# Rotary sums made in place on 128 partitions and carried to the heads' rows by DMAs, on one Trainium2 core

## The chip, the cores and the metric

One core of a Trainium2 chip. The metric is the device time of one execution in microseconds. The kernel before takes 1430.77 us, the median of 3 runs (1430.03 to 1432.64).

## The reference, cut to what matters

One inference step of a two-layer streaming encoder, 512 prompt frames and 32 sample frames of width 1024. In each layer a normalised input is projected by one matrix to the inputs of three parallel head groups: retention (4 heads of 64), gated linear attention (4 heads of 64) and band attention (8 heads of 64). Their outputs are joined, projected back and added; an MLP of width 4096 follows. The change touches only the rotary embedding of retention's q and k:

```python
def rotary(x, pos):
    half = HEAD_DIM // 2
    ...
    x1, x2 = x[..., :half], x[..., half:]
    return jnp.concatenate([x1 * cos - x2 * sin, x1 * sin + x2 * cos], axis=-1)

qa = rotary(heads(qa), pos)
ka = rotary(heads(ka), pos) * scale
```

## The kernel before

Activations lie transposed: features on the partitions, the T = 544 frames (512 + 32) along the row. A weight matrix is cut into units of 128 output features, 100 for each layer. Each unit's 512 KB are loaded by SyncE's queue (SP) into one of four buffers `raw`; ScalarE (ACT) makes the high part `whi` (`split(n)`, L467), VectorE (DVE) the low part `wlo` (`rest(n)`, L767), and TensorE (PE) makes 48 matmuls (hi by hi, hi by lo, lo by hi; 8 slices of the contraction; two halves of 272 frames) into two PSUM banks. `unit_out(n)` on DVE then reads the banks. DVE, ACT and PE each run the written order of `SLOTS`: slot (n, half) is half a unit of projection products on PE, and the small matmuls of the head groups (`PE_STEPS`) are put ahead of or between them. On each engine instructions run in the order in which they are written, and all order between engines is by semaphores written by hand. `begin(n)` on PE waits for `w_lo` of unit n and for the reads of units up to n - 2.

Units 6 and 7 (`RK`) are retention's k, units 8 and 9 (`RQ`) its q. The weight columns are permuted so that the first unit of a pair holds the first halves (x1) of all four heads, 32 rows for each head, and the second unit the second halves (x2). `unit_out(RK)` writes `rot[0]` = x1 cos and `rot[1]` = x1 sin, `unit_out(RK + 1)` writes `sq[0]` = x2 sin and `sq[1]` = x2 cos, all on 128 partitions. `rotary(first, g)` (L852 to L864) then makes the sums, and because the matmuls of the heads want each head's 64 features on adjacent rows (`rk`, `rq`, two heads for each g), it does so in four DVE operations of 32 partitions for each g: 8 for k after `rest(9)` (slots (8, 0) and (8, 1)), 8 for q after `rest(11)` (slots (10, 0) and (10, 1)), so 16 for each layer. Since `rot` and `sq` are used again for q, `unit_out(RQ)` waits for `rot_ready` 2. The readers of `rk` and `rq`: the step ("diag", RET) at PE's slot (11, 1), which waits for `rot_ready` 4; DVE's decay scaling (L961, L963); the transposes and the state steps after it.

DVE's work around it, in its written order: slot (8, 0): `unit_out(7)`, the last level of the gated linear attention (GLA), `rest(9)` and rotary of k; slot (9, 0): `unit_out(8)` (writes `rot`), `rest(10)`; slot (9, 1): step ("kv", GLA), 16 state updates (L1017) and 2 for the sample frames (L1023); slot (10, 0): `unit_out(9)` (writes `sq`), `rest(11)`, rotary of q; slot (10, 1): the adds of ("out", GLA) (L1031); slot (11, 0): `unit_out(10)`, ("out_s", GLA), `rest(12)`; slot (11, 1): ("diag", RET), L947 on. PE's step ("out", GLA) at slot (10, 1) takes all four side banks; bank 2 of them comes free with `state_s_ready`, after the second L1023.

SP issues the loads in order: `load(m)` waits for `rest(m - 4)`. Between loads stand other transfers (`between`): before `load(15)` `states_out(GLA)` (4 stores of 32 KB), before `load(16)` `state_in(RET)` (2 loads of 32 KB that wait for DVE's `outs_dve`), and so on; `band_in(0)` waits for `rot_ready` 4.

Of the kernel before, what the change touches and what calls it, by code (L numbers as in the profile page):

```python
# [11 lines left out]
T = TP + TS  # L12
# [24 lines left out]
ALU, ACT = mybir.AluOpType, mybir.ActivationFunctionType  # L37
# [4 lines left out]
GK, GQ, GV, RK, RQ, RV, AQ, GATE = 0, 2, 4, 6, 8, 10, 12, 24  # L42

GLA, RET = 0, 1
# [28 lines left out]
    _steps[(12, 0)] = _steps[(12, 0)] + [("gn", GLA)]  # L73
    _steps[(15, 0)] = [("gn", RET)]
GN_PARTS = [(0, 8), (8, 20)]
ROTARY = {(8, 0): (RK, 0), (8, 1): (RK, 1), (10, 0): (RQ, 0), (10, 1): (RQ, 1)}
for _u in range(4):
    _b = 16 + 3 * _u
    DVE_STEPS[(_b + 1, 0)] = [("norm", _u, 0), ("score", _u, 1)]
# [7 lines left out]
for _steps in (DVE_STEPS, ACT_STEPS):  # L87
# [10 lines left out]
    qk_dve=6, pe_lev=6, lev_read=6, pe_diag=2, diag_read=2, qe_act=1, qe_dve=1, kd_arg=1, kd_act=1, kd_ready=1,  # L98
    dec_ready=1, pe_tok=4, tok_read=4, pe_kv=2, state_ready=32, state_s_ready=4, pe_out=2, out_act=2, out_dve=4,
    pe_out_s=2, outs_act=2, outs_dve=4, centred=2, gn_var=2, gn_act=6, gn_done=4, pe_back=2, back_read=4,  # L100
    rot_ready=4, ret_scaled=2, o_cleared=1, s_cleared=1, part_hi=8, part_lo=8, pe_heads=4, heads_act=4,
    pe_score=8, score_dve=32, max_ready=8, exp_done=8, norm_done=8, pe_score_s=4, score_s_dve=8, exp_s=4,
    norm_s=4, pe_turn=8, turned=24, pe_turn_s=4, turned_s=4, pe_pv=4, pv_act=4, pv_dve=4, pe_pv_s=4, pvs_act=4,
    pvs_dve=4, gate_act=8, gate_dve=8, cat_dve=4, cat_hi=4, cat_lo=4, relu_ready=32, z_hi=32, z_lo=32,
# [43 lines left out]
def hybrid_encoder(nc, x, wu, w_low, a2, small, bias, bias_s, st_ret, st_gla, ck, cv,  # L148
# [3 lines left out]
    with ctx:  # L152
# [22 lines left out]
        sq = [sb(f"sq{i}", [P, T]) for i in range(2)]  # L175
# [35 lines left out]
        rot = [at("rot0", [P, T], arena + Z), at("rot1", [P, T], arena + Z + 4 * T)]  # L211
        rv, rk, rq = (at(n, [P, PW], arena + (2 + i) * Z) for i, n in enumerate(["rv", "rk", "rq"]))
# [33 lines left out]
        sems = {}  # L246

        def sem(name):
# [17 lines left out]
            "pe_diag", "diag_read", "qe_act", "qe_dve", "kd_arg", "kd_act", "kd_ready", "dec_ready",  # L266
            "pe_tok", "tok_read", "pe_kv", "state_ready", "state_s_ready", "pe_out", "out_act", "out_dve",
            "pe_out_s", "outs_act", "outs_dve", "centred", "gn_var", "gn_act", "gn_done",
            "pe_back", "back_read", "rot_ready", "ret_scaled", "o_cleared", "s_cleared",
            "part_hi", "part_lo", "pe_heads", "heads_act", "pe_score", "score_dve", "max_ready", "exp_done", "norm_done",  # L270
            "pe_score_s", "score_s_dve", "exp_s", "norm_s", "pe_turn", "turned", "pe_turn_s", "turned_s",
            "pe_pv", "pv_act", "pv_dve", "pe_pv_s", "pvs_act", "pvs_dve",
# [7 lines left out]
        with nc.Block() as block:  # L280
            @block.sync
            def _(sp):
# [12 lines left out]
                for layer in range(L):  # L295
                    nth = counter(layer)
# [19 lines left out]
                    def band_in(u):  # L316

                        if u == 0:
                            sp.wait_ge(sems["rot_ready"], nth("rot_ready", 4))
                            sp.wait_ge(sems["pe_tok"], nth("pe_tok", 4))  # L320
                        for p in range(2):
                            if u >= 1:
                                sp.wait_ge(sems["score_dve"], nth("score_dve", 4 * (2 * (u - 1) + p + 1)))
                            sp.dma_start(Bh[p][:, :], bias[layer, 2 * u + p, :, :]).then_inc(sems[f"bias_in{p}"], 16)
                        if u >= 2:
                            sp.wait_ge(sems["pe_score_s"], nth("pe_score_s", u - 1))
                            sp.wait_ge(sems["pe_pv_s"], nth("pe_pv_s", u - 1))
                        cols = slice(u * P, (u + 1) * P)
                        sp.dma_start(kct[u % 2][:, :], ck[layer, u, :, :]).then_inc(sems[f"cache_in{u % 2}"], 16)
                        sp.dma_start(cvb[u % 2][:, :, :], cv[layer, :, cols].rearrange("(j p) c -> p j c", p=P)) \  # L330
                            .then_inc(sems[f"cache_in{u % 2}"], 16)
                        if u >= 1:
                            sp.wait_ge(sems["score_s_dve"], nth("score_s_dve", 2 * u))
                        sp.dma_start(Bs[:, :], bias_s[layer, u, :, :]).then_inc(sems["bias_s_in"], 16)

                    def states_out(kind):
                        sp.wait_ge(sems["state_ready"], nth("state_ready", 16 * (kind + 1)))
# [6 lines left out]
                    def rows_out(u):  # L344
# [9 lines left out]
                    load(RAW)  # L354
                    state_in(GLA)

                    between = {11: (states_out, GLA), 12: (state_in, RET), 14: (states_out, RET), 15: (band_in, 0),
                               17: (rows_out, 0), 18: (band_in, 1), 20: (rows_out, 1), 21: (band_in, 2),
                               23: (rows_out, 2), 24: (band_in, 3), 26: (rows_out, 3)}
                    for n in range(RAW + 1, N_IN + RAW):  # L360
# [388 lines left out]
            def _(dve):  # L749
# [7 lines left out]
                for layer in range(L):  # L757
                    nth = counter(layer)
# [51 lines left out]
                    def unit_out(n):  # L810
# [4 lines left out]
                            dve.wait_ge(sems["rstd_ready"], nth("rstd_ready", 1))  # L815

                        if n == RQ:
                            dve.wait_ge(sems["rot_ready"], nth("rot_ready", 2))

                        def out(dst, by):  # L820
                            return nc.vector.tensor_tensor(dst, src, by, ALU.mult)
# [1 line left out]
                        if n in (GQ, GQ + 1):  # L823
                            d = gq[:, (n - GQ) * T:(n - GQ + 1) * T].rearrange("p (a b) -> p a b", a=2)
                            ins = nc.vector.scalar_tensor_tensor(d, src, HD ** -0.5, halves(rstd), ALU.mult, ALU.mult)
                        elif n in (RK, RQ):
# [4 lines left out]
                            ins = out(halves(rot[1]), halves(nt[1]))  # L831
                        elif n in (RK + 1, RQ + 1):
                            link(out(halves(sq[0]), halves(nt[1])))
                            ins = out(halves(sq[1]), halves(nt[0]))
                        elif n >= GATE:
                            ins = out(halves(G[n - GATE]), halves(rstd))
                        elif n >= AQ:
# [4 lines left out]
                            if which == 0:  # L842
                                ins = nc.vector.scalar_tensor_tensor(d, src, HD ** -0.5, halves(rstd), ALU.mult, ALU.mult)
                            else:
                                ins = out(d, halves(rstd))
# [3 lines left out]
                                      halves(rstd))  # L849
                        ins.then_inc(sems["unit_read"], 1)  # L850

                    def rotary(first, g):  # L852

                        dst = rk if first == RK else rq
                        if layer and first == RK and g == 0:
                            for s in range(2):
                                dve.wait_ge(sems[f"stored{s}"], nth(f"stored{s}", 0))
                        dve.wait_ge(sems["unit_read"], nth("unit_read", first + 2))
                        c = slice(g * T, (g + 1) * T)
                        for p in range(2):  # L860
                            s32 = slice(32 * (2 * g + p), 32 * (2 * g + p) + 32)
                            nc.vector.tensor_tensor(dst[64 * p:64 * p + 32, c], rot[0][s32, :], sq[0][s32, :], ALU.subtract)
                            ins = nc.vector.tensor_tensor(dst[64 * p + 32:64 * p + 64, c], rot[1][s32, :],
                                                          sq[1][s32, :], ALU.add)  # L864
                        ins.then_inc(sems["rot_ready"], 1)

                    def square_sums(a, b):
                        return nc.vector.reduce_sum(gst[0][:, a:b], osq[:, a * HD:b * HD].rearrange("p (a c) -> p a c", c=HD),
# [277 lines left out]
                    for n, half in SLOTS:  # L1146
                        if half == 0 and n >= 3 and n != 15:
                            unit_out(n - 1)
                        rest_first = n == 14
                        if half == 0 and rest_first:  # L1150
                            rest(n + 1)
                        for st in DVE_STEPS.get((n, half), []):
                            stage(st)
                        if (n, half) == (15, 0):
                            unit_out(n - 1)
                        if half == 0 and not rest_first:
                            rest(n + 1)
                        if (n, half) in ROTARY:
                            rotary(*ROTARY[(n, half)])
                        if half == 0 and n > GATE + 1:  # L1160
                            gate_rest(n - GATE - 2)
                        if half == 1 and n > GATE:
                            gate_min(n - GATE - 1)
                            gate_mul(n - GATE - 1)
# [116 lines left out]
            def _(pe):  # L1281
# [6 lines left out]
                for layer in range(L):  # L1288
# [47 lines left out]
                    def stage(st, quarter=0):  # L1336
# [26 lines left out]
                        elif what == "diag":  # L1363
# [1 line left out]
                            q, k = ((gq, gk), (rq, rk))[kind]  # L1365
                            pe.wait_ge(sems["unit_read"], nth("unit_read", GQ + 2)) \
                                if kind == GLA else \
                                pe.wait_ge(sems["rot_ready"], nth("rot_ready", 4))
                            take(0, 1, 2, 3)
                            for p, g, c in chunks():  # L1370
                                r, o = slice(64 * p, 64 * p + 64), g * T + c * CH
# [411 lines left out]
```

## Time and profile before

| | us |
|---|---|
| median of 3 runs (range) | 1430.77 (1430.03 to 1432.64) |
| the profiled execution | 1430.05 |
| its span, first to last instruction | 1428.2 |
| PE busy | 1400.8 (98%) |
| DVE busy | 773.3 (54%) |
| ACT busy | 521.0 (36%) |
| POOL busy | 147.2 (10%) |

All times are microseconds from the start of the span unless marked ns. L862 is line 862 of the kernel before. PEld is PE's weight load, which runs beside its matmuls; SPq is SP's queue as it issues DMAs. Matmuls are pipelined: in a steady stream one starts every 0.12 to 0.13 us though each is shown for 0.29 us. Both layers have the same stretch, layer 0 from about 85 to 120 us and layer 1 from about 785 to 820 us; the first is read unless it says otherwise.

### The profile page before, as it was taken

The page shows a single profiled execution, that of the slowest core. Times are in us where ns is not written, and L with a number is a line of the kernel's source. Part 1 is how long each engine was busy: PE and PEld are TensorE (multiplying, and loading weights), DVE is VectorE, ACT ScalarE, POOL GpSimd, SP SyncE. Part 2 cuts the span into 40 slices and gives each one's busy share as a digit, 9 for nine tenths or more (in the row PEclk, how much of TensorE's full clock was granted, in tenths as well). Part 3 has the DMA queues.
Part 4 walks back from the last instruction along what each step waited for, and adds up shares of the span by engine and source line. Part 5 has one row for each costly group of instructions (what it writes and reads, how often), then busy time and mean ns, then how long its engine had stood idle before and what let it go on. Part 6 is the DMA issues. An engine that isn't in the chain of part 4 may idle for free.

```text
span 1428.2 us, 28637 instructions
## 1 busy us (share of the span) xinstructions
PE 1400.8 (98%) x12590; PEld 1359.4 (95%) x12590; DVE 773.3 (54%) x1224; ACT 521.0 (36%) x859; POOL 147.2 (10%) x107
## 2 busy tenths in 40 slices
PE   8999999999999999999999999999999999999996
PEld 8999889899999999999998999889999999999996
DVE  6797766744434334344767967765453443433433
ACT  5323556633213223123332236565332231321331
POOL 0200000031020110200202000001301102002012
PEclk9999999999999999999999999999999999999998
DMA  6123333222222222222221223422222222222211
GB/s 231 59 59 101 98 111 100 75 99 85 85 88 89 90 89 89 89 89 89 78 73 46 66 83 117 137 89 75 89 89 90 89 86 84 86 86 89 89 60 63
DMA packets 50635, 127.82 MB, mean 90 GB/s; under 512 B 8400, under 2 KB 17744, under 8 KB 50512
## 3 DMA queue, kind: packets, MB, share of 16 engines
q1 hardware_dynamic: 50224, 125.44, 27.0%
q8 instruction: 100, 1.64, 0.5%
q10 hardware_dynamic: 288, 0.55, 0.1%
q14 instruction: 23, 0.19, 0.0%
HBM read 118.77 MB, written 7.21 MB: 88 GB/s over the span
## 4 chain that ended last, share of the span: by engine, by line
PE 87%; DVE 5%; ACT 3%; issue 3%; POOL 1%; DMA 0%; POOLq 0%; SPq 0%; DVEq 0%; ACTq 0%
PE PS L1302 85%; ACT whi L467 1%; POOL h L435 1%; PE PS L1537 1%; ACT Pr L594 1%; PE PS L1416 1%; DVE Pr L1084 0%; DMA raw<-in_wu 0%; DVE F L889 0%; DVE gb L935 0%; DVE Pr L1096 0%; DVE sq L1203 0%; DVE wlo L767 0%; ACT xhi L470 0%; DVE O L877 0%
## 5 line engine op out<-in xcount | busy, mean ns | idle before, releaser
L1302 PE MATMUL PS<-xhi,whi 128*128 128x272 f32 x1920 | 562.9, 293 | 3.5 <-DVE wlo L767 2.6
L1302 PE MATMUL PS<-xhi,wlo 128*128 128x272 f32 x1920 | 555.2, 289 | 0.0
L1302 PE MATMUL PS<-xlo,whi 128*128 128x272 f32 x1920 | 552.7, 288 | 0.0
L767 DVE TENSOR_TENSOR wlo<-raw,whi 128x1024 fp32r<-128x1024 f32 x200 | 251.6, 1258 | 386.0 <-ACT whi L467 385.3
L467 ACT ACTIVATE whi<-raw 128x1024 fp32r<-128x1024 f32 x200 | 211.6, 1059 | 558.6 <-PE PS L1302 554.0
L1302 PEld LDWEIGHTS PS<-xhi,whi 128*128 128x128 f32 x1920 | 361.3, 188 | 15.5 <-issue 9.0
L1302 PE MATMUL PS<-zhi,wlo 128*128 128x272 f32 x1280 | 370.6, 290 | 0.0
L1302 PE MATMUL PS<-zhi,whi 128*128 128x272 f32 x1280 | 368.5, 288 | 0.4 <-DVE wlo L767 0.4
L1302 PE MATMUL PS<-zlo,whi 128*128 128x272 f32 x1280 | 368.5, 288 | 0.0
L1302 PEld LDWEIGHTS PS<-xlo,whi 128*128 128x128 f32 x1920 | 361.8, 188 | 0.2
L1302 PEld LDWEIGHTS PS<-xhi,wlo 128*128 128x128 f32 x1920 | 361.2, 188 | 0.0
L1302 PEld LDWEIGHTS PS<-zhi,whi 128*128 128x128 f32 x1280 | 241.0, 188 | 0.9 <-DVE wlo L767 0.9
L1302 PEld LDWEIGHTS PS<-zlo,whi 128*128 128x128 f32 x1280 | 241.1, 188 | 0.0
L1302 PEld LDWEIGHTS PS<-zhi,wlo 128*128 128x128 f32 x1280 | 240.8, 188 | 0.0
L435 POOL TENSOR_TENSOR h<-h,sq 128x544 f32<-128x544 f32 x62 | 89.3, 1441 | 653.1 <-DVE sq L1203 653.1
L662 ACT ACTIVATE zhi<-nt 128x544 fp32r<-128x544 f32 x64 | 42.2, 659 | 90.6 <-DVE nt L1192 90.6
L1195 DVE TENSOR_TENSOR zlo<-nt,zhi 128x544 fp32r<-128x544 f32 x64 | 50.0, 781 | 46.4 <-ACT zhi L662 46.4
L1203 DVE TENSOR_TENSOR sq<-PS,r 128x544 f32<-128x544 f32 x62 | 44.5, 718 | 20.6 <-PE PS L1302 14.5
L594 ACT ACTIVATE Pr<-Pr,mx 128x128 f32<-128x128 f32 (+1 forms) x64 | 35.2, 552 | 34.9 <-DVE mx L1089 34.9
L1192 DVE SCALAR_TENSOR_TENSOR nt<-PS,nt 128x544 f32<-128x544 f32 x64 | 46.0, 718 | 0.0
L426 POOL TENSOR_SCALAR ssum<-sq 128x544 f32<-128x544 f32 x2 | 2.4, 1183 | 416.9 <-ACT sq L651 416.9
L659 ACT ACTIVATE nt<-PS 128x544 f32<-128x544 f32 x64 | 38.8, 606 | 0.0
(226 smaller groups left out, 1083.0 us busy)
## 6 DMA issues: line engine op xcount, KB each, us to landing
raw<-in_wu SPq DMA_DIRECT2D x199, 512.0 KB, 3.5
Bh<-in_bias SPq DMA_DIRECT2D x16, 256.0 KB, 3.9
h<-in_x SPq DMA_DIRECT2D x8, 272.0 KB, 6.1
out_k_t<-att_k SPq DMA_DIRECT2D x8, 272.0 KB, 4.3
out_y_t<-y SPq DMA_DIRECT2D x8, 272.0 KB, 2.7
kct<-in_ck SPq DMA_DIRECT2D x8, 256.0 KB, 3.2
cvb<-in_cv SPq DMA_DIRECT2D x8, 256.0 KB, 5.0
out_v_p<-vtk SPq DMA_DIRECT2D x8, 256.0 KB, 2.2
```

What stands on the lines that cost most here:

```text
L435: nc.gpsimd.tensor_tensor(h[:, m, :], h[:, m, :], sq[m % 2][:, :], ALU.add) \
L467: nc.scalar.activation(whi[n % SPL][:, :], raw[n % RAW][:, :], ACT.Copy).then_inc(sems["w_hi"], 1)
L594: ins = nc.scalar.activation(r, r, ACT.Exp, bias=mx[:, p, i:i + 1], accum_out=rs[:, p, i:i + 1])
L659: nc.scalar.activation(halves(r), PS[:, 2 * (n % 2):2 * (n % 2) + 2, 0:HT], ACT.Relu) \
L662: nc.scalar.activation(zhi[:, k, :], r[:, :], ACT.Copy).then_inc(sems["z_hi"], 1)
L767: nc.vector.tensor_tensor(wlo[n % SPL][:, :], raw[n % RAW][:, :], f32(whi[n % SPL][:, :]), ALU.subtract).then_inc(sems["w_lo"], 1)
L1192: nc.vector.scalar_tensor_tensor(halves(r), PS[:, 2 * (n % 2):2 * (n % 2) + 2, 0:HT], 0.0, halves(r), ALU.max, ALU.mult).then_inc(sems["un ...
L1195: nc.vector.tensor_tensor(zlo[:, k, :], r[:, :], f32(zhi[:, k, :]), ALU.subtract) \
L1203: nc.vector.tensor_tensor(halves(sq[m % 2]), PS[:, 2 * (n % 2):2 * (n % 2) + 2, 0:HT], halves(r2), ALU.mult).then_inc(sems["unit_read"], 1)
L1302: return nc.tensor.matmul(out, lhsT, rhs, start=start, stop=stop, skip_group_check=True)
L1416: nc.tensor.transpose(PS[:, M0 + g, i * P:(i + 1) * P], src[:, g * T + i * P:g * T + (i + 1) * P], ident[:, :])
L1537: last = nc.tensor.transpose(PS[:, M0 + b, c:c + P], Pr[p][:, P_OFF[i] + j * P:P_OFF[i] + (j + 1) * P], ident[:, :])
```

## The change

Rotary of k is one call in slot (8, 0) and rotary of q one call in slot (10, 0). Each is two DVE operations on all 128 partitions, in place in `rot[0]` and `rot[1]`, that count `rot_sum`. A new step of SP, `heads_apart`, waits for `rot_sum` and issues 8 DMAs from SBUF to SBUF, each of 32 partitions by 544 elements of float32 (68 KB), from `rot[x]` to `rk` or `rq`; each adds 16 to `rot_in`. For k it stands before `load(14)`, for q before `load(16)`; `state_in(RET)` moves from before `load(16)` to before `load(17)`. `unit_out(RQ)` on DVE now waits for `rot_in` 128 (all of k's carries), ("diag", RET) on PE and `band_in(0)` on SP for `rot_in` 256. The wait for `stored0` and `stored1` in layer 1 moves from DVE to SP.

```diff
-ROTARY = {(8, 0): (RK, 0), (8, 1): (RK, 1), (10, 0): (RQ, 0), (10, 1): (RQ, 1)}
+ROTARY = {(8, 0): RK, (10, 0): RQ}
...
+                    def heads_apart(first):
+
+                        sp.wait_ge(sems["rot_sum"], nth("rot_sum", 1 + (first == RQ)))
+                        if layer and first == RK:
+                            for s in range(2):
+                                sp.wait_ge(sems[f"stored{s}"], nth(f"stored{s}", 0))
+                        dst = rk if first == RK else rq
+                        for g in range(2):
+                            for p in range(2):
+                                for x in range(2):
+                                    sp.dma_start(dst[64 * p + 32 * x:64 * p + 32 * x + 32, g * T:(g + 1) * T],
+                                                 rot[x][32 * (2 * g + p):32 * (2 * g + p) + 32, :]).then_inc(sems["rot_in"], 16)
...
-                    between = {11: (states_out, GLA), 12: (state_in, RET), 14: (states_out, RET), 15: (band_in, 0),
+                    between = {10: (heads_apart, RK), 11: (states_out, GLA), 12: (heads_apart, RQ), 13: (state_in, RET), 14: (states_out, RET), 15: (band_in, 0),
...
                         if n == RQ:
-                            dve.wait_ge(sems["rot_ready"], nth("rot_ready", 2))
+                            dve.wait_ge(sems["rot_in"], nth("rot_in", 16 * 8))
...
-                    def rotary(first, g):
-
-                        dst = rk if first == RK else rq
-                        if layer and first == RK and g == 0:
-                            for s in range(2):
-                                dve.wait_ge(sems[f"stored{s}"], nth(f"stored{s}", 0))
+                    def rotary(first):
+
                         dve.wait_ge(sems["unit_read"], nth("unit_read", first + 2))
-                        c = slice(g * T, (g + 1) * T)
-                        for p in range(2):
-                            s32 = slice(32 * (2 * g + p), 32 * (2 * g + p) + 32)
-                            nc.vector.tensor_tensor(dst[64 * p:64 * p + 32, c], rot[0][s32, :], sq[0][s32, :], ALU.subtract)
-                            ins = nc.vector.tensor_tensor(dst[64 * p + 32:64 * p + 64, c], rot[1][s32, :],
-                                                          sq[1][s32, :], ALU.add)
-                        ins.then_inc(sems["rot_ready"], 1)
+                        nc.vector.tensor_tensor(rot[0][:, :], rot[0][:, :], sq[0][:, :], ALU.subtract)
+                        nc.vector.tensor_tensor(rot[1][:, :], rot[1][:, :], sq[1][:, :], ALU.add) \
+                            .then_inc(sems["rot_sum"], 1)
...
                                 if kind == GLA else \
-                                pe.wait_ge(sems["rot_ready"], nth("rot_ready", 4))
+                                pe.wait_ge(sems["rot_in"], nth("rot_in", 16 * 16))
```

## Rows read from the trace of the kernel before

**Rows 1.** The page: busy time (share of the span, instructions), and the chain's shares by engine.
```profile
PE 1400.8 (98%) x12590; PEld 1359.4 (95%) x12590; DVE 773.3 (54%) x1224; ACT 521.0 (36%) x859; POOL 147.2 (10%) x107
...
PE 87%; DVE 5%; ACT 3%; issue 3%; POOL 1%; DMA 0%; POOLq 0%; SPq 0%; DVEq 0%; ACTq 0%
```

**Rows 2.** Waits of PE and PEld, 60 to 170 us: total us, times, longest.
```profile
PE PS L1488 <- DVE O L1059: 1.1, 1, 1.1
...
PEld PS L1302 <- DVE wlo L767: 0.2, 1, 0.2
PEld PS L1416 <- DVE rk L963: 0.2, 1, 0.2
PEld PS L1302 <- DVE Ps L992: 0.2, 1, 0.2
```

**Rows 3.** Timeline of DVE: start us, us, operation, [idle before, releaser].
```profile
89.29 1.22 DVE L767 TENSOR_TENSOR wlo<-raw,whi 128x1024 fp32r<-128x1024 f32 x1
90.43 0.71 DVE L862 TENSOR_TENSOR rk<-rot,sq 32x544 f32<-32x544 f32 x1
...
96.37 1.49 DVE L821 TENSOR_TENSOR rot<-PS,nt 128x544 f32<-128x544 f32 x2
97.77 1.22 DVE L767 TENSOR_TENSOR wlo<-raw,whi 128x1024 fp32r<-128x1024 f32 x1
...
101.97 0.47 DVE L1023 SCALAR_TENSOR_TENSOR Ss<-Ss,dec,PS 128x64 f32<-128x64 f32 x2
...
104.88 0.71 DVE L862 TENSOR_TENSOR rq<-rot,sq 32x544 f32<-32x544 f32 x1
...
108.00 1.29 DVE L1031 TENSOR_TENSOR O<-PS,O 128x512 f32<-128x512 f32 x2 [0.23 <-ACT O L538]
...
112.26 0.72 DVE L821 TENSOR_TENSOR rv<-PS,rstd 128x544 f32<-128x544 f32 x1
...
116.32 0.69 DVE L947 TENSOR_TENSOR Pm<-PS,dm_sb 128x512 f32<-128x512 f32 x1 [0.57 <-PE PS L1302]
```

**Rows 4.** Groups of DVE's instructions: count, busy us, mean ns, idle before.
```profile
L1139 DVE TENSOR_TENSOR G<-G,sq 128x544 f32<-128x544 f32 x8 | 5.8, 725 | 1.2 <-DVE G L1133 0.5 <-ACT sq L695 0.2
...
L863 DVE TENSOR_TENSOR rk<-rot,sq 32x544 f32<-32x544 f32 x8 | 5.7, 718 | 0.1
```

**Rows 5.** Timeline of PE and PEld at the edges of its steps.
```profile
99.83 0.19 PEld L1302 LDWEIGHTS PS<-xhi,whi 128*128 128x128 f32 x1
...
102.84 0.29 PE L1302 MATMUL PS<-xhi,wlo 128*128 128x272 f32 x1
103.06 0.45 PE L1302 MATMUL PS<-vtok,Pm 64*64 64x64 f32 x8
...
114.10 1.03 PE L1302 MATMUL PS<-rq,rk 64*64 64x64 f32 x28
```

**Rows 6.** Timeline of SP's queue: issues of DMAs.
```profile
102.53 0.35 SPq L341 DMA_DIRECT2D out_gla_p<-S  x1
102.92 0.43 SPq L342 DMA_DIRECT2D out_gla_s<-Ss  x1
103.39 0.44 SPq L341 DMA_DIRECT2D out_gla_p<-S  x1
```

**Rows 7.** DMA issues: count, KB of each, median us from issue to landing.
```profile
raw<-in_wu SPq DMA_DIRECT2D x199, 512.0 KB, 3.5
out_k_t<-att_k SPq DMA_DIRECT2D x8, 272.0 KB, 4.3
...
out_gla_p<-S SPq DMA_DIRECT2D x4, 32.0 KB, 1.5
...
out_v_s<-vtk SPq DMA_DIRECT2D x8, 16.0 KB, 2.0
```

**Rows 8.** Windows of 1 us; the last two columns are DMA share and GB/s.
```profile
93.00:94.00 1.00, 1.00 (x10) 1.00 (x10) 0.97 (x2) 0.74 (x3) 0.00 (x0) 1.00 0.75 307
94.00:95.00 1.00, 1.00 (x11) 1.00 (x10) 0.97 (x3) 0.00 (x0) 0.00 (x0) 1.00 0.05 20
```

**Rows 9.** Timeline of PE in layer 1, the first matmul of ("out", GLA).
```profile
802.77 0.44 PE L1302 MATMUL PS<-vtok,Pm 64*64 64x64 f32 x7
```

More of the change, by code:

```diff
@@ L100 @@
     pe_out_s=2, outs_act=2, outs_dve=4, centred=2, gn_var=2, gn_act=6, gn_done=4, pe_back=2, back_read=4,
-    rot_ready=4, ret_scaled=2, o_cleared=1, s_cleared=1, part_hi=8, part_lo=8, pe_heads=4, heads_act=4,
+    rot_sum=2, rot_in=256, ret_scaled=2, o_cleared=1, s_cleared=1, part_hi=8, part_lo=8, pe_heads=4, heads_act=4,
     pe_score=8, score_dve=32, max_ready=8, exp_done=8, norm_done=8, pe_score_s=4, score_s_dve=8, exp_s=4,
@@ L268, in hybrid_encoder @@
             "pe_out_s", "outs_act", "outs_dve", "centred", "gn_var", "gn_act", "gn_done",
-            "pe_back", "back_read", "rot_ready", "ret_scaled", "o_cleared", "s_cleared",
+            "pe_back", "back_read", "rot_sum", "rot_in", "ret_scaled", "o_cleared", "s_cleared",
             "part_hi", "part_lo", "pe_heads", "heads_act", "pe_score", "score_dve", "max_ready", "exp_done", "norm_done",
@@ L318, in band_in @@
                         if u == 0:
-                            sp.wait_ge(sems["rot_ready"], nth("rot_ready", 4))
+                            sp.wait_ge(sems["rot_in"], nth("rot_in", 16 * 16))
                             sp.wait_ge(sems["pe_tok"], nth("pe_tok", 4))
@@ L1158, in _ @@
                         if (n, half) in ROTARY:
-                            rotary(*ROTARY[(n, half)])
+                            rotary(ROTARY[(n, half)])
                         if half == 0 and n > GATE + 1:
```

## The prediction

> **What bounds the kernel now.** I read the page's busy times and its chain first: PE is busy 98% of the span, its weight loads 95%, and 87% of the chain that ended last is PE's own [rows 1]. So time comes off only where PE waits, and is added wherever PE is made to wait. Next I read PE's waits around the place of the change: from 60 to 170 us PE lacks only 1.1 us (L1488, for DVE's L1059 at 154 us), and PEld three times 0.2 us [rows 2]. None of these is a wait for `rk` or `rq` as rotary leaves them; the 0.2 us of L1416 is for the scaling by decay, a chain that starts at PE's own diag step. DVE is another matter: it works almost without a gap from 85 us until 115.8 us, and is level with PE again only at 116.32, where L947 has stood idle 0.57 us for PE [rows 3]. DVE is thus late in this stretch, but its lateness reaches PE almost nowhere. The question is not what DVE saves but how late the two new waits are against PE's dates.
>
> **The sums.** An operation on 32 partitions takes 718 ns; one on 128 partitions with both inputs in SBUF, the shape of the new sums, 725 ns [rows 4]. Rotary goes from 8 x 0.72 = 5.7 us to 2 x 0.72 = 1.4 us, so 4.3 us less each time, and 4 x 4.3 = 17 us less DVE busy time in two layers (773 to about 756). On PE's path this is worth nothing by itself: DVE has no successor there that starts sooner than PE lets it, because from 116.32 on DVE waits for PE in either case. As a bound from below the gain can't exceed what PEld lacks of DVE in this stretch, 0.2 + 0.2 + 0.2 = 0.6 us a layer [rows 2], 1.2 us in all; I take 0, since two of the three stand before the rotary sums or behind PE's own diag step.
>
> **The wait of DVE for k's carries.** This is the term that decides. Before, `unit_out(8)` started at 96.37, directly behind the last of the 8 operations [rows 3]. After:
> - `rest(9)` and the start of the sums stay: 90.43. The sums end at 90.43 + 1.44 = 91.87, and SP, which has just issued `load(13)`, can start at about 91.90.
> - SP issues 8 DMAs. The second follows the first by 0.39 us, later ones by 0.47 us [rows 6]: the eighth is issued at 91.90 + 0.39 + 6 x 0.475 = 95.14.
> - Landing of a transfer from SBUF to SBUF isn't in the trace. The nearest rows: 1.5 us for a store of 32 KB, 2.0 us for a store from 32 partitions, 3.5 us for a load of 512 KB, 4.3 us for a store of 272 KB [rows 7]. I take 2.0 (same partitions, small), with 1.5 and 4.3 as ends. The eighth lands at 97.14 (96.64 to 99.44).
>
> So `unit_out(8)` starts d = 0.8 us later than before (0.3 to 3.1), although DVE has 4.3 us less to do: its gain has become idle time, and somewhat more.
>
> Behind the waiting `unit_out(8)` are queued on DVE `rest(10)`, the 18 state updates, `unit_out(9)` and `rest(11)`. Who waits for them, and with what slack:
> - PE's `begin(10)` needs `rest(10)`, which ended at 97.77 + 1.22 = 98.99; PEld starts the unit at 99.83 [rows 3, 5]. Slack 0.8 us.
> - PE's ("out", GLA) takes bank 2, which is free when the L1023 pair ends, 101.97 + 0.47 = 102.44. The last matmul ahead of it starts at 102.84, and the step at 103.06 [rows 3, 5]. The 0.22 between these is also there ahead of steps that wait for nothing, so the slack is 103.0 - 102.44, about 0.55 us with some 0.05 for the semaphore taken off. This one binds.
>
> PE's stall is then d - 0.55: 0.25 us in each layer for d = 0.8, 0 for d = 0.3, 2.55 for d = 3.1. A shift here stays, since PE is never ahead of itself again. Layer 1 has the same stretch (its step starts at 802.77 [rows 9]; that layer's L1023 pair ends as far ahead of it), so 0.5 us in all (0 to 5.1).
>
> **q's carries.** `rest(11)` ended and the sums began at 104.88 [rows 3]; with d they begin at 105.7 and end at 107.1. `load(15)` and the 4 stores of `states_out` are out by then. SP issues 8 DMAs, the last at 107.15 + 3.24 = 110.4; at 2.0 us they land at 112.4. PE's diag wants them at 114.10 [rows 5]: slack 1.7 us, so nothing. With 4.3 us of landing and d = 3.1, they land at 117.0, when PE itself has slipped to 116.65: 0.35 us more a layer, which makes the upper end 5.8 us. On DVE the L1031 adds at 108.00 wait for ACT [rows 3] and lie behind sums that now end before them.
>
> **The rest of what moves.** `load(14)` is now issued behind the 8 carries, at 99.8 at the latest (it waits for `rest(10)` in any case, formerly 99.0), and `load(16)` behind q's, which are issued by 111; it waits for `rest(12)`, now as before, and that comes at 113 to 115.8. Loads are four units ahead and take 3.5 us [rows 7], so ACT's split isn't reached. `state_in(RET)` goes out after `load(16)`, not before; its data are wanted at about 132 us by the RET state update, 15 us later. `band_in(0)` waits for carries that PE has needed 20 us earlier. The wait for `stored` in layer 1 is for stores of layer 0, long done. The 32 carries move 2.2 MB beside 127.8 MB. All of it is hidden by that distance; cost 0.
>
> **Sum.** Profiled execution 1430.05 + 0 (sums) + 0.5 (k's carries) + 0 (q's carries) + 0 (rest) = 1430.55. That execution lies 0.7 below the median of the runs shown, and carried to the median the forecast is 1431.3 us: no change that can be measured, 0.2% of this time (2.9 us) being about the least that a measurement can tell from none.
>
> **Rivals.**
> 1. *The carries are served slowly, and queue behind the load.* `load(13)` is issued at 90.54, and its data keep the DMA engines busy until 94.05 [rows 8]; by then five carries are issued. A load reaches 307 GB/s in a full microsecond. If transfers of 32 partitions get half of that, the 544 KB of eight carries take 3.6 us from 94.05, to 97.7, and with about 0.7 us of completion (half of the 1.5 us of a small store) the last lands at 98.4: d = 2.0, stall 1.45 a layer, 2.9 us in all, 1433.7. For it speaks that the load's data do lie just ahead; against it, that the eighth carry is issued a microsecond after the load is through. The Trainium skill has such a rule (SBUF — State Buffer, "Door 1: The DMA port swizzle"): a transfer over partitions 0 to 31 reaches 8 of the 16 DMA ports, 189 GB/s at 1 MiB where all partitions give 328. By that page's rate the eight take 2.9 us from 94.05, so an estimate of 97.0 for the data and of 97.7 for the landing: 0.8 us stall a layer, a total of 1.6 us. No transfer of 32 partitions of this size is in the trace, so no row can say whether it holds.
> 2. *Slower: every carry lands like a large transfer.* If the time from issue to landing is 3.4 us or more, whatever the size, the end is at 98.5 or later, d above 2.0, and both layers together lose more than 2.9 us: at 4.3 us of landing 5.8 us, 1436.6. It decides from 3.4 us on. Against it: all stores of small size land in 1.5 to 2.0 us [rows 7]; for it: a store of rows of 2176 bytes, as the carries have, took 4.3.
> 3. *Faster.* DVE's early finish would have to reach PE. Between 85 and 116 us PE lacks no more than 0.6 us of anything from DVE [rows 2], so 1.2 us at most, which would be 1429.6, if k's carries also cost nothing (landing at 1.5 us, d = 0.3). This can't be told from no change.
> 4. *The change doesn't do what it says*: the DVE operations on 128 partitions cost more than 0.72 us. [Rows 4] all but rule it out; DVE would have to lose 4 us more to matter.
>
> **How the numbers follow.** Forecast (0 to 1.5 us more) 0.58; rival 1 (1.5 to 3.3 more) 0.20; rival 2 0.12; rival 3, a little faster, 0.09; rival 4 0.01. Half of rival 1's upper part, some 0.05, passes 2.9 us. Faster by over 0.2% would need a mechanism that no row shows, or a shift of medians: 0.03. Slower: 0.12 + 0.05 = 0.17. Same: 0.80. The range reaches from rival 3, less a part of the 0.7 us by which the lowest run lies under the median, 1429.3, to the upper part of rival 1, 1434.2; what it leaves out is rival 2 and some of both tails.
>
> **What would show it.** DVE idle of 4 to 6 us ahead of L821 `rot` (`unit_out(8)`), with a DMA `rk<-rot` as releaser, at about 92 and 792 us; rot at 96.7 to 97.7 and not 96.37; the carries 0.47 us apart on SP; a wait of PEld or PE of about 0.25 us at the first `vtok,Pm` matmul of each layer for DVE's L1023, and none at the diag step; DVE busy near 756 us. The prediction is wrong if a carry takes over 3.4 us to land, if SP issues such a DMA in more than 0.6 us, or if PE has a wait for `rot_in`.

## The result

The changed kernel takes 1436.25 us, the median of 6 runs (1435.14 to 1438.51); before, 6 runs on the same chip gave 1430.44 (1430.03 to 1432.64). The ratio is 1.0039, 95% interval 1.0026 to 1.0052: 5.6 us slower (the medians themselves differ by 5.8). In a second set, 7 runs of the changed kernel gave 1435.11 against 1430.56, ratio 1.0032 (1.0021 to 1.0043). The forecast was 1431.3 with a range to 1434.2: both the size and "no change" were wrong. The time lies where rival 2 had put its own, though it came about in another way.

The page of the kernel after, the lines that answer to [rows 1]:

```profile
PE 1403.5 (98%) x12590; PEld 1361.9 (95%) x12590; DVE 756.2 (53%) x1200; ACT 521.0 (36%) x859; POOL 147.2 (10%) x107
...
PE 85%; DVE 6%; issue 3%; ACT 3%; POOL 1%; DMA 1%; SPq 1%; POOLq 0%; DVEq 0%; ACTq 0%
```

DVE's busy time fell by 17.1 us, as worked out, and SP's queue and a DMA have come into the chain, with 1% each. The profiled execution took 1435.70 us, its span 1433.9. PE's waits from 60 to 170 us, which answer to [rows 2] (total, times, longest):

```profile
PE PS L1307 <- DVE wlo L780: 1.9, 1, 1.9
PE PS L1493 <- DVE O L1064: 1.3, 2, 1.1
PE PS L1307 <- DVE Ss L1028: 0.3, 1, 0.3
```

The first and the last are new; the middle one (L1064, the L1059 of the kernel before) was there. L780 is the `rest` of the kernel before (L767), L1028 its L1023. The timeline of DVE in the kernel after, which answers to [rows 3]:

```profile
90.06 1.22 DVE L780 TENSOR_TENSOR wlo<-raw,whi 128x1024 fp32r<-128x1024 f32 x1
91.19 0.72 DVE L868 TENSOR_TENSOR rot<-rot,sq 128x544 f32<-128x544 f32 x1
91.83 0.72 DVE L869 TENSOR_TENSOR rot<-rot,sq 128x544 f32<-128x544 f32 x1
100.15 1.48 DVE L834 TENSOR_TENSOR rot<-PS,nt 128x544 f32<-128x544 f32 x2 [7.60 <-DMA rk<-rot]
101.55 1.22 DVE L780 TENSOR_TENSOR wlo<-raw,whi 128x1024 fp32r<-128x1024 f32 x1
...
119.64 0.69 DVE L952 TENSOR_TENSOR Pm<-PS,dm_sb 128x512 f32<-128x512 f32 x1 [1.82 <-PE PS L1307]
```

The stretch begins with `rest(9)`, at 90.06 here and at 89.29 before. So I count from `rest(9)`: the first q unit is read (`rot<-PS`) 10.09 us after it; before it was 96.37 - 89.29 = 7.08. DVE is d = 3.01 us late, not 0.8. The diag step's result (`Pm<-PS`), which only follows PE, comes 29.58 us after `rest(9)`; before it was 27.03. The stretch costs 2.55 us. In layer 1 the same three instants are:

```profile
792.28 1.22 DVE L780 TENSOR_TENSOR wlo<-raw,whi 128x1024 fp32r<-128x1024 f32 x1
...
801.57 1.48 DVE L834 TENSOR_TENSOR rot<-PS,nt 128x544 f32<-128x544 f32 x2 [6.80 <-DMA rk<-rot]
...
821.06 0.69 DVE L952 TENSOR_TENSOR Pm<-PS,dm_sb 128x512 f32<-128x512 f32 x1 [1.83 <-PE PS L1307]
```

d = 9.29 - 7.08 = 2.21, and the cost 28.78 - 27.07 = 1.71 us. Together these are 4.26 of the 5.7 us of span. Where d comes from is in SP's queue, which answers to [rows 6], and in the chain, whose rows are start, us, what:

```profile
92.58 5.05 SPq L346 DMA_DIRECT2D rk<-rot  x8
```

```profile
96.39 0.59 SPq L346
96.98 0.04 issue
97.03 3.03 DMA rk<-rot
```

An issue takes 0.59 us, 0.635 from one to the next, where stores had taken 0.43 and 0.475. (In layer 1 the eight take 5.22 us, with one pause of 0.36 us between two of them.) And the last carry of layer 0 needs 3.03 us to land, while the median of all is the 2.0 us that I had assumed (an answer to [rows 7]):

```profile
rk<-rot SPq DMA_DIRECT2D x16, 68.0 KB, 2.0
rq<-rot SPq DMA_DIRECT2D x16, 68.0 KB, 2.0
```

### The profile page after: what moved, and what is told of

Its sections match the earlier page's. It is cut to its first block, busy times and chain, and to the rows that moved or that the text cites. A ratio compares the mean times of both kernels' runs of the same rounds, so it can differ in the third digit from the quotient of the medians.

```text
span 1433.9 us, 28645 instructions
## 1 busy us (share of the span) xinstructions
PE 1403.5 (98%) x12590; PEld 1361.9 (95%) x12590; DVE 756.2 (53%) x1200; ACT 521.0 (36%) x859; POOL 147.2 (10%) x107
## 4 chain that ended last, share of the span: by engine, by line
PE 85%; DVE 6%; issue 3%; ACT 3%; POOL 1%; DMA 1%; SPq 1%; POOLq 0%; DVEq 0%; ACTq 0%
PE PS L1307 83%; ACT whi L480 1%; POOL h L448 1%; PE PS L1542 1%; ACT Pr L607 1%; DVE wlo L780 1%; SPq L346 1%; DVE Pr L1089 0%; DVE S L1022 0%; DMA rk<-rot 0%; DVE F L894 0%; DVE gb L940 0%; DMA sm<-in_small 0%; ACT xhi L483 0%; DVE Pr L1101 0%
## 5 line engine op out<-in xcount | busy, mean ns | idle before, releaser
L780 DVE TENSOR_TENSOR wlo<-raw,whi 128x1024 fp32r<-128x1024 f32 x200 | 251.6, 1258 | 385.9 <-ACT whi L480 385.2
```

Source lines behind the costliest of these rows:

```text
L780: nc.vector.tensor_tensor(wlo[n % SPL][:, :], raw[n % RAW][:, :], f32(whi[n % SPL][:, :]), ALU.subtract).then_inc(sems["w_lo"], 1)
```

## The experiments

The theory (A): DVE's wait for k's eight carries makes its later work late, and PE waits for that; the largest part of DVE's wait is the number of issues times 0.63 us. Against it stood B (part of the loss is at the start and the end of the program), C (the carries' traffic, or their issues ahead of the loads, cost in themselves) and the prediction's rival 1 (the carries queue behind the load's data).

### The kernel before, once more

No edit.

> The kernel before, unchanged, to see how far two programs with the same text differ, and whether its start and end vary. In the profiles of before and after, 4.25 us of the 5.7 us of span lie in the two rotary stretches; 0.8 us lie ahead of 40 us and 0.65 us behind 1400 us, where the granted clock was 0.87 (10 to 20 us) and 0.73 (from 1400 us) against 1.00 and 0.77. Theory A (the wait for k's carries is the whole cause, the rest is variation of the profiled executions): a new profile of before shows starts or ends that differ by several tenths of a us again; time 1430.0 to 1432.6. Theory B (start and end are part of the change): start and end come out as in the first profile to 0.1 us.

1430.79 us (11 runs, 1429.79 to 1431.50), ratio 0.9998 (0.9989 to 1.0006). Start and end came out within 0.3 us of the first profile; `rest(9)` at 89.41. This by itself decides little about B; `q_only`, below, decides more.

### The wait taken away, the carries kept

```diff
+        rotq = [qkv[1][0], qkv[1][2]]
...
-                            dve.wait_ge(sems["rot_in"], nth("rot_in", 16 * 8))
...
-                            link(out(halves(rot[0]), halves(nt[0])))
-                            ins = out(halves(rot[1]), halves(nt[1]))
+                            ro = rot if n == RK else rotq
+                            link(out(halves(ro[0]), halves(nt[0])))
+                            ins = out(halves(ro[1]), halves(nt[1]))
```

> As after, but q's sums lie in two tiles of their own (the band attention's q and v tiles of the second set, idle at this time), so unit_out of the first q unit waits for no carry; all 32 carries are still made. Theory A (the wait of DVE for k's eight carries makes the loss, by rest(10) and the state updates arriving late at PE): DVE starts that unit_out some 1 us after the sums, not 8; both waits of PE in each stretch vanish; 1430.4 to 1431.8 us. Theory C (the carries themselves cost: their transfers, or their issues on SP that hold up the loads of weights): the loss of 5.8 us stays, 1435 to 1437. Theory B: 1.4 us of it stays, 1432.

1430.79 us (11 runs, 1429.65 to 1431.47), ratio 0.9997 (0.9988 to 1.0006). The whole loss is gone. Here `rotq`, two tiles of the band attention that are idle at this time, takes q's products and sums. DVE and SP of this kernel:

```profile
89.65 1.22 DVE L781 TENSOR_TENSOR wlo<-raw,whi 128x1024 fp32r<-128x1024 f32 x1
...
92.06 0.72 DVE L832 TENSOR_TENSOR att_q<-PS,nt 128x544 f32<-128x544 f32 x1
...
97.33 3.16 DVE L1022 SCALAR_TENSOR_TENSOR S<-S,dec,PS 128x64 f32<-128x64 f32 x16 [2.66 <-PE PS L1307]
...
116.72 0.69 DVE L952 TENSOR_TENSOR Pm<-PS,dm_sb 128x512 f32<-128x512 f32 x1 [1.84 <-PE PS L1307]
```

```profile
92.17 5.05 SPq L347 DMA_DIRECT2D rk<-rot  x8
```

The eight carries take SP the same 5.05 us, but nobody on the path waits for them. DVE is ahead of PE now (2.66 us idle before the state updates, when it had none), and the diag result comes 27.07 us after `rest(9)`, as before (27.03). C falls with this: all 32 carries are there and cost nothing that the interval can show. DVE's 17 us less work also bring nothing: this kernel is not faster than the one before.

### Only k, only q

`k_only` makes q's rotary by the eight operations on 32 partitions again, `q_only` k's:

```diff
-ROTARY = {(8, 0): RK, (10, 0): RQ}
...
-                            rotary(ROTARY[(n, half)])
+                            (rotary if ROTARY[(n, half)] == RK else rotary32)(ROTARY[(n, half)])
```

(for `q_only` with RQ; `rotary32` is the old `rotary` for both g in one call.)

> Only k is summed in place and carried; q's rotary is made by the eight operations on 32 partitions, as before. Theory A: the whole loss is here, 1435.5 to 1437, PE's waits in each stretch as in after (2.5 and 1.7 us). Theory C: half of the loss, about 1433.3, since half of the carries are left.

> Only q is summed in place and carried; k's rotary is made as before. Theory A: no loss, 1430.0 to 1431.5; the last carry lands before PE's diag step, with some 1 to 2 us to spare (in after: last issue at 114.4, landed near 116.6, diag at 117.4). Theory C: half of the loss, about 1433.3.

`q_only`: 1430.24 us (11 runs, 1429.71 to 1432.05), ratio 0.9999 (0.9990 to 1.0007). q's carries cost nothing, as A says. `k_only`: 1442.9 us (5 runs, 1441.69 to 1446.58), ratio 1.0087 (1.0075 to 1.0100), a loss of 12 us, twice what was expected. PE's waits in it from 88 to 125 us:

```profile
PE PS L1324 <- DVE O L1053: 2.6, 1, 2.6
PE PS L1324 <- DVE wlo L781: 2.1, 1, 2.1
PE PS L1324 <- DVE Ss L1045: 0.3, 1, 0.3
```

The last two are the known ones. The first is new and was of my making: I had put all eight operations for q ahead of the adds of the "out" step, where the kernel before has four ahead of them and four behind. With this mended (`k_only_split`, the call cut in two, (10, 0) and (10, 1)):

> As k_only, but q's eight operations stand in two halves around the adds of L1053, as in the kernel before; in k_only I had put all eight ahead of the adds, and PE waited 2.6 us a layer for these adds. Only the first two waits of PE should be left: as after, 1434.5 to 1436.5 us, which would say that q's in-place sums are worth nothing in after. If they are worth something once DVE is late, it is above after: 1437 to 1442.

1435.56 us (5 runs, 1434.42 to 1436.21), ratio 1.0033 (1.0020 to 1.0045), and the wait for the adds is gone. So k alone makes the loss, and whether q's sums take 1.4 or 5.7 us makes no difference of a size that these intervals can show. The miss of `k_only` tells something all the same: with DVE 3.1 us late in layer 0 and 2.0 in layer 1, eight operations ahead of the adds cost PE 2.6 us a layer.

One thing more is in the profile of `k_only_split`. Right after PE's wait of 2.2 us in layer 0 its matmuls start 0.227 us apart from 104.2 to 107.0 us and not 0.125, and the granted clock (the third value from the end) is that of the lower level, 1.2 GHz:

```profile
104.00:105.00 1.00, 1.00 (x7) 1.00 (x6) 1.00 (x6) 0.00 (x0) 0.00 (x0) 0.54 0.90 324
105.00:106.00 1.00, 1.00 (x6) 1.00 (x6) 1.00 (x6) 0.00 (x0) 0.00 (x0) 0.50 0.32 127
```

That stretch costs 3.99 us with d = 3.31, some 1.1 us more than the lateness alone gives in the other profiles (the table below). In `k_only` the clock fell to 0.66 from 820 to 825 us, behind the wait for the adds in layer 1, where the stretch cost 1.5 us more than its waits. In the profiles of after, its repetition, `wide` and `before_load`, with waits of 1.8 to 2.5 us in the same place, it stayed at 1.00. So such a wait can be followed by a loss of clock of about 1 us, and need not be; the length of the wait alone does not decide it here.

### DVE late without a DMA

```diff
+                            if n == RQ:
+                                for t in (qkv[1][0], qkv[1][2], qkv[0][0], qkv[0][2]):
+                                    nc.vector.tensor_tensor(t[:, :], nt[0][:, :], nt[1][:, :], ALU.mult)
```

in the kernel before.

> The kernel before with four more DVE products of 128x544 (0.65 us apart, both inputs in SBUF, results unused) just ahead of the reads of the first q unit: d = 2.6 to 2.9 us and not one DMA more. Theory A (only DVE's lateness counts): the same two waits of PE as in k_only, whose d was 3.15 us, and the same third one, for L1053's adds ahead of the sample frames' step, each shorter by the difference of d: 4.8 us a layer, 9.6 in two, some 1440 us. Theory C (the carries' traffic adds to it): clearly less, since no carry is made: under 1436.

1434.72 us (8 runs, 1433.50 to 1435.86), ratio 1.0029 (1.0019 to 1.0039). The number expected was wrong, since it rested on `k_only` with its third wait; the mechanism is clearest here. The trace of this kernel:

```profile
89.33 1.22 DVE L767 TENSOR_TENSOR wlo<-raw,whi 128x1024 fp32r<-128x1024 f32 x1
...
98.95 1.48 DVE L821 TENSOR_TENSOR rot<-PS,nt 128x544 f32<-128x544 f32 x2
...
118.44 0.69 DVE L950 TENSOR_TENSOR Pm<-PS,dm_sb 128x512 f32<-128x512 f32 x1 [0.30 <-PE PS L1305]
```

```profile
PE PS L1305 <- DVE wlo L767: 1.5, 1, 1.5
PE PS L1305 <- DVE Ss L1026: 0.3, 1, 0.3
```

d = 9.62 - 7.08 = 2.54 and the stretch costs 29.11 - 27.03 = 2.08 us (2.55 and 2.16 in layer 1), with the same two waits as the kernel after. The stretches cost 4.24 us together, and the medians differ by 4.5. No carry is made: DVE's lateness is enough.

### Two queues

Half of the carries (p = 1) are issued by GpSimd's queue, with a semaphore of their own:

```diff
+                    for dst, count in ((rk, 1), (rq, 2)):
+                        pool.wait_ge(sems["rot_sum"], nth("rot_sum", count))
+                        for g in range(2):
+                            for x in range(2):
+                                nc.gpsimd.dma_start(dst[64 + 32 * x:96 + 32 * x, g * T:(g + 1) * T],
+                                                    rot[x][32 * (2 * g + 1):32 * (2 * g + 1) + 32, :]).then_inc(sems["rot_in2"], 16)
```

> As after, but half of the carries (p = 1) are issued by GpSimd's queue, which is idle at this time, and half by SP. In after an issue takes SP 0.59 us, 0.63 us from one to the next, eight of them 5.0 us. Theory A: SP's four are issued by 94.4 on before's time scale and land by 96.0; GpSimd's price for an issue is not in any trace so far. If it is 0.6 us or less, d is about 0 and the loss is gone, 1430 to 1431.5; at 1.0 us and 2.5 us of landing d is about 1.5, 1432.5. If the loss stays at 5 us or more the issue rate was not the cause, or GpSimd takes over 1.5 us for each.

1431.25 us (11 runs, 1429.78 to 1432.63), ratio 1.0005 (0.9997 to 1.0014). A twelfth execution took 2266.52 us and is left out; its mean granted clock was 0.554, where the others had 0.993 to 0.995, and why it was so low stays open. From `rest(9)` to the first q unit:

```profile
90.97 1.22 DVE L786 TENSOR_TENSOR wlo<-raw,whi 128x1024 fp32r<-128x1024 f32 x1
...
98.26 1.48 DVE L840 TENSOR_TENSOR rot<-PS,nt 128x544 f32<-128x544 f32 x2 [4.80 <-DMA rk<-rot]
```

SP issues its four in 2.51 us, GpSimd its four in 2.33. d = 7.29 - 7.08 = 0.21 us (0.39 in layer 1), and the stretches cost nothing: the wait is there, 4.80 us of it, but within the slack. Four issues fewer in a row are 2.5 us, while the median landing rose from 2.0 to 2.8 us (SP's) and 2.6 us (GpSimd's), so a part of the gain was given back. The number of issues in a row on one queue is thus the largest term, and halving it is enough.

### What an issue costs

`wide` moves 136 elements of all 128 partitions with each carry, so that the rows don't come to the heads' places and only its times are of use; `sixteen` cuts each carry in two along the row (its edit is shown):

```diff
-                                    sp.dma_start(dst[64 * p + 32 * x:64 * p + 32 * x + 32, g * T:(g + 1) * T],
-                                                 rot[x][32 * (2 * g + p):32 * (2 * g + p) + 32, :]).then_inc(sems["rot_in"], 16)
+                                    for c in (0, HT):
+                                        sp.dma_start(dst[64 * p + 32 * x:64 * p + 32 * x + 32, g * T + c:g * T + c + HT],
+                                                     rot[x][32 * (2 * g + p):32 * (2 * g + p) + 32, c:c + HT]) \
+                                            .then_inc(sems["rot_in"], 16)
```

> As after, but each of the 8 carries takes 136 elements of all 128 partitions, so the same 68 KB each and the same count; the rows do not come to the heads' places (that part of the computation is changed). If the 32-partition shape is what makes an issue take 0.59 us, it is 0.43 here, as for SP's stores, the last issue is 1.1 us sooner and the stretch loses about 1.1 us a layer less; if a transfer from SBUF to SBUF costs that, 0.59 stays.

> As after, but each carry is cut into two of 272 elements: 16 transfers of 34 KB for k and 16 for q, the same bytes. If an issue costs by the instruction, SP needs 10.1 us for k's, the last is issued at 101.3 on before's scale and lands at 103.3: d = 7, PE's first two waits grow by 4.5 to 5 us a layer, some 1445 to 1448. If it costs by the bytes, the time is that of after, 1436.

SP's queue in `wide`, then in `sixteen`:

```profile
92.66 5.05 SPq L347 DMA_DIRECT2D rk<-rot  x8
```

```profile
92.60 11.36 SPq L347 DMA_DIRECT2D rk<-rot  x16
```

The shape is not the cause: 5.05 us for eight in `wide` too (1434.72 us in one run, d = 3.41 and 2.09, costs 2.96 and 1.58). Nor are the bytes: half the size costs as much for each issue (10.05 us for sixteen in layer 1; 11.36 in layer 0, some more). So among these three shapes the price is by the instruction. `sixteen` took 1459.63 us in one run, more than expected: d = 8.14 and 6.87, but q's carries are late for PE's diag step as well, which before had slack:

```profile
PE PS L1309 <- DVE wlo L782: 7.1, 1, 7.1
PE PS L1309 <- DMA rq<-rot: 3.7, 1, 3.7
```

### The load ahead of the carries

```diff
-                    between = {10: (heads_apart, RK), 11: (states_out, GLA), ...
+                    between = {9: (heads_apart, RK), 11: (states_out, GLA), ...
```

> As after, but k's carries are issued ahead of load(13), not behind it; that load then goes out some 6 us later. In after the carries of layer 0 landed 2.0 to 2.4 us after their issue, but the last 3.0 us, and in layer 1 the first three 2.5 to 2.7 us. Rival 1 of the prediction (the carries queue behind the load's data): every carry lands in 2.0 us, d is 2.1 us in both layers, the stretches lose 3.3 us, 1434 or less. If the load ahead does not matter: as after, 1435 to 1436.5. If load(13) is now late for its split: more than after.

1435.70 us (5 runs, 1433.33 to 1436.21), ratio 1.0032 (1.0020 to 1.0045): as after. The last carry in the chain of layer 0, and of layer 1, of this kernel:

```profile
96.60 3.62 DMA rk<-rot
```

```profile
799.94 2.02 DMA rk<-rot
```

With no load ahead of it the last carry of layer 0 took 3.62 us, even more than after's 3.03, and d was 3.60 and 2.18. Rival 1 falls as the account of the late landing. Its mechanism is there, but on carries that nobody waits for: in layer 1 of after the first three carries, issued while the load's data came in, landed in 2.5 to 2.7 us, and in 2.0 us here.

What goes with the late landing is another row. DMA queues of the kernel after, in the 3 us in which the last carry of layer 0 lands (packets, MB, share of 16 engines):

```profile
q1 hardware_dynamic: 96, 0.14, 18.6%
q8 instruction: 1, 0.02, 2.3%
```

One packet of instructions takes 2.3% of 16 engines in 3 us, so 0.023 x 16 x 3 = 1.1 us of one engine. Such a packet stands in this place of layer 0 in six profiles with a last landing of 2.9 to 3.6 us; in layer 1 of the same six, where the last carry lands in 2.0 us, none does. The two go together in size as well. The packet's own time comes from its share of 16 engines in the half microsecond in which it starts, where it is counted whole: 12.4% x 16 x 0.5 us = 0.99 us in `after_again`, 21.0% and 1.68 us in `before_load`.

```profile
q8 instruction: 1, 0.02, 12.4%
```

```profile
q8 instruction: 1, 0.02, 21.0%
```

| kernel, layer 0 | packet, us of one engine | last carry's landing, us |
|---|---|---|
| after_again | 0.99 | 2.87 |
| after | 1.13 | 3.03 |
| k_only | 1.22 | 3.15 |
| wide | 1.34 | 3.42 |
| k_only_split | 1.39 | 3.33 |
| before_load | 1.68 | 3.62 |

In all six the landing is later than 2.05 us by nearly the packet's time. In a seventh profile, `own_tiles`, the packet took 0.94 us and the last carry 3.8, but there a load of 512 KB was issued right behind it. That the carry's part on that engine waits for the packet fits these rows but is an inference; no run moved the packet.

### The changed kernel, once more

> The changed kernel, unchanged. In the profiled runs so far a stretch loses d - 0.46 us (d: how much later than before DVE reads the first q unit, counted from the rest(9) ahead of it): after 3.01 and 2.21 give 2.55 and 1.71, late_dve 2.54 and 2.55 give 2.08 and 2.16, two_queues 0.21 and 0.39 give 0 and 0. Theory A with these numbers: both stretches together lose 4 to 5 us again and the median is 1434.5 to 1435.5; what is above that is variation of the carries' landing from run to run, or of the start (granted clock 0.87 or 1.00 from 10 to 20 us). If the median is again 5.8 above before's and the stretches show 4.3, some 1.5 us lie outside of the stretches and stay open.

1435.11 us (7 runs, 1433.88 to 1436.50). d = 2.86 and 2.21, costs 2.68 and 1.73, together 4.4 us against 4.55 between the medians of this set. The first of the two contains 0.2 us of PE's wait for a carry of q at the diag step, which the first profile does not have. In the first set the medians differ by 5.8 us where its profile shows 4.3; the intervals of the two sets overlap. What remains above the stretches is 0.1 to 1.5 us, and is left open. A fall of the clock like that of `k_only_split` would have the size: the six executions of the first set had mean granted clocks of 0.992 to 0.994, the seven of the second 0.993 to 0.996. Neither profile shows such a fall in the stretches, so this is not shown.

Stretches with carries or delays, in one table (layer 0; layer 1; us). `k_only` and `sixteen`, which have a third wait, and a wait for q's carries, on top, are not in it:

| kernel | d | cost | d - cost |
|---|---|---|---|
| after | 3.01; 2.21 | 2.55; 1.71 | 0.46; 0.50 |
| after_again | 2.86; 2.21 | 2.68; 1.73 | 0.18; 0.48 |
| late_dve | 2.54; 2.55 | 2.08; 2.16 | 0.46; 0.39 |
| wide | 3.41; 2.09 | 2.96; 1.58 | 0.45; 0.51 |
| before_load | 3.60; 2.18 | 3.47; 1.69 | 0.13; 0.49 |
| k_only_split | 3.31; 1.98 | 3.99; 1.49 | -0.68; 0.49 |
| two_queues | 0.21; 0.39 | 0; 0 | |

A stretch costs d less some 0.46 us. The exceptions are all in layer 0: `after_again` and `before_load` have 0.2 us at the diag step on top, where PE waits for a carry of q, and `k_only_split` has the fall of the clock.

About B: the granted clock of PE from 10 to 20 us, the third value from the end of a window's row, was 1.00 in before. In after and in `q_only` it was lower:

```profile
10.00:20.00 10.00, 10.00 (x71) 9.92 (x71) 10.00 (x17) 8.03 (x14) 0.00 (x0) 0.87 1.05 393
```

```profile
10.00:20.00 10.00, 9.31 (x61) 9.24 (x62) 10.00 (x16) 8.34 (x14) 0.00 (x0) 0.83 1.05 394
```

`rest(9)` stood at 90.06 and 90.94 against 89.29. But `q_only` is as fast as before in the median of 11 runs. The start varies between executions by more than what is in question, so the 0.77 us that lie ahead of layer 0's stretch in after's profile are not put to the change's account. The other 0.7 us of its span lie behind layer 1's stretch, towards the end of the program; in the second profile of the same kernel that part is 0.8 us shorter than in before, so it is not put to the change either. B has no support left, though a few tenths of a microsecond can't be excluded.

## Why the prediction was wrong, point by point

- **What bounds the kernel; DVE's saving is worth nothing on PE's path.** Right. DVE's busy time came out at 756.2 us as forecast, and with the wait gone (`own_tiles`) the kernel is 0.9997 of the one before.
- **The sums.** Right: 0.72 us each, 0.64 from the first's start to the second's.
- **SP's issues.** This is the step that failed, the price of an issue in the term of k's carries. I took 0.475 us between issues from stores of 128 partitions [rows 6], and kept no second value; the issue of a transfer from SBUF to SBUF takes 0.635. Seven steps took 4.45 us in place of the 3.24 in the sum, 1.2 us more; in layer 1, with its pause, 4.63 us, 1.4 more. I had given both ends to the landing but none to the issue, though the trace showed no issue of this kind either. The prediction named an issue of more than 0.6 us among what would make it wrong, without pricing it.
- **The landing.** 2.0 us was right for most carries and for the last one of layer 1; the last of layer 0 took 3.03. It was inside the bounds given for it (1.5 to 4.3), but the stated range left the upper ones out: its end, 1434.2, is reached when d is about 2.3 us in both layers, and d came out at 3.01 and 2.21.
- **The slack.** 0.55 us was forecast, 0.46 measured, at the same place: the L1023 pair and bank 2, with `begin(10)` taking the larger part of the wait since it comes first on PE. With the measured d (3.01 and 2.21) and my slack the sum would have been 2.46 + 1.66 = 4.1 us, and the stretches show 4.26. The mechanism was right, and the term of k's carries was mis-sized: 0.5 us forecast, 4.3 measured.
- **The sum of two shortages.** The forecast's d of 0.8 us had already used up the slack of 0.55, so all that came on top counted in full, once for each layer: 1.2 + 1.4 us of issues and 1.0 us of landing in layer 0 make 3.6 of the 3.8 us missed.
- **q's carries.** Worked out as free with 1.7 us to spare; they are free or cost 0.2 us (a wait of PE for `rot_in` at the diag step in layer 0 of one of the two profiles of the changed kernel, and in `before_load`), because DVE and with it the sums were later than forecast. `q_only` shows no loss.
- **The rest of what moves.** Right: no load was late in the stretches; `state_in(RET)` behind `load(16)` made no wait.
- **Rivals.** Rival 2 (slower) gave the right sign with the wrong cause: it wanted a landing of 3.4 us or more, and in the changed kernel the latest took 3.03 and most 2.0; what it said of a d above 2 us holds. Rival 1's load ahead is refuted by `before_load`. The rule of the Trainium skill cited beside it, that a transfer over 32 partitions reaches half of the ports (SBUF — State Buffer, "Door 1: The DMA port swizzle"), can't be seen here: carries of all 128 partitions (`wide`) landed in the same median of 2.0 us, and with 68 KB every 0.635 us, 110 GB/s, the issues set the pace, below the 189 GB/s of that rule. A chance of 0.17 for slower was too small, because both terms of the wait, the issue and the landing, came from rows of another kind of transfer, and only the landing had been given bounds.

## What to carry to other kernels

A wait for several DMAs issued in a row costs the number of issues times the time of one issue, plus the landing of the last; price the issue from a transfer of the same kind (SBUF to SBUF here 0.635 us, stores 0.475), and give it bounds if the trace has none. Give the last landing bounds too: it is one transfer, not the median, and here it took 2.0 to 3.6 us. When an engine off the path is slowed down, look for the smallest slack among all that is queued behind the new wait: from there on every tenth counts in full, once for each layer. If a transfer's source must be written again soon, there are two ways to try: another tile for the next writer took the transfers off the path here, and splitting the issues over two queues brought them within the slack; the saving on DVE, for which PE does not wait, brought nothing in either case.

## What the runs showed of the hardware that I had not expected

- The issue of a DMA from SBUF to SBUF holds SP for 0.59 to 0.60 us, whether it moves 68 KB or 34 KB, 32 partitions or 128 (after, `sixteen`, `wide`); a store of 128 partitions 0.43.
- The last of k's carries landed 0.9 to 1.6 us later than most of its fellows in layer 0 of six profiles, in which a packet of instructions (1.0 to 1.7 us of one DMA engine) stood in the same place, beginning 0.6 to 0.8 us after the last issue began; the longer the packet, the later it landed, with one exchange of neighbours. In layer 1 of these six there was no such packet, and it landed in 2.0 us.
- In `sixteen` PE's granted clock fell in or after its long waits. The windows of 100 to 110 us, with the wait of 7.1 us in it, and of 130 to 140 us, after the 3.7 us at the diag step (the third value from the end is the clock):

```profile
100.00:110.00 10.00, 2.95 (x17) 2.73 (x16) 4.67 (x15) 1.06 (x1) 0.00 (x0) 0.73 0.20 49
...
130.00:140.00 10.00, 10.00 (x72) 9.83 (x69) 6.70 (x20) 2.69 (x6) 0.00 (x0) 0.73 0.01 2
```

  A mean of 0.73 is a time at 1.2 GHz and the rest at 2.4 GHz. The two stretches of that kernel cost 13.5 and 11.7 us, 2.1 and 1.8 us more than d and the diag waits give (8.1 + 3.7 and 6.9 + 3.5, less the slack of 0.46 us). A shorter wait can be followed by the same: 2.2 us in `k_only_split`, and not 1.9 us in the kernel after, whose clock stays at 1.00 in this stretch.
